# Five edits of order in a decoder layer: attention's beginning, halves of x, local maxima, up projection, merge

## What is computed

```python
z = x @ w_in
qa, ka, va, qi, ki, wi, qb, kb, vb, gate = jnp.split(z, SPLIT_POINTS, axis=-1)
ya = sparse_attention(...)          # 8 heads of 64, top-256 keys of an index score, T5 bias
yb = sliding_window_attention(...)  # 8 heads, 2 key-value heads, window 128, sinks, T5 bias
g = jax.nn.sigmoid(gate)
mix = (g[..., :D] * (ya @ w_pa) + g[..., D:] * (yb @ w_pb)) @ w_o
x = layer_norm(ALPHA * x + mix, ln1_g, ln1_b)
u = x @ w_up                        # 6144 columns: 3072 gate, 3072 value
c = conv_b + causal depthwise convolution of width 3 of u along the positions
x = layer_norm(ALPHA * x + (jax.nn.gelu(c[gate]) * c[value]) @ w_down, ln2_g, ln2_b)
```

## Time and profile before

| | |
|---|---|
| time, median of 3 runs | 3416.0 us (3415.43 to 3418.09) |
| profiled execution | 3410.55 us, span 3408.8 us |
| TensorE busy | 3252.1 us, 95% |
| VectorE busy | 2460.3 us, 72% |
| ScalarE busy | 1661.9 us, 49% |
| GpSimd busy | 1012.2 us, 30% |
| mean granted TensorE clock | 0.984 of full |

### The profile page before, as it was taken

The page is one execution under the profiler, slowest core; times in us unless marked ns, Lnnn a source line. Parts: engine busy times, 40 slices in busy tenths (PEclk is TensorE's granted clock), DMA queues, the critical chain, the costliest instruction groups (busy, mean ns, idle before and its releaser), DMA issues.

```text
span 3408.8 us, 40734 instructions
## 1 busy us (share of the span) xinstructions
PE 3252.1 (95%) x14552; PEld 2581.5 (76%) x14552; DVE 2460.3 (72%) x3632; ACT 1661.9 (49%) x2289; POOL 1012.2 (30%) x592
## 2 busy tenths in 40 slices
PE   7999989996899999999999999999999999999998
PEld 5788878874566666667877787777788888888887
DVE  5899999956566656446666799999899998343344
ACT  5669888215566676663222344444544444321211
POOL 1012232324466666650021144332233331000000
PEclk9999999997999999999999999999999999999999
DMA  6323333444232221035565322223322223533522
GB/s 172 59 75 99 99 105 99 134 162 96 74 77 70 60 65 49 7 110 193 176 247 185 119 87 100 105 101 133 108 92 75 93 87 128 197 103 117 173 96 95
DMA packets 219187, 376.81 MB, mean 111 GB/s; under 512 B 30573, under 2 KB 119933, under 8 KB 211182
## 3 DMA queue, kind: packets, MB, share of 16 engines
q1 hardware_dynamic: 217934, 369.86, 34.0%
q0 software_dynamic: 1056, 4.36, 0.3%
HBM read 276.24 MB, written 97.80 MB: 110 GB/s over the span
## 4 chain that ended last, share of the span: by engine, by line
PE 48%; DVE 16%; issue 6%; ACT 5%; DMA 2%; POOL 1%; SPq 1%; DVEq 0%; ACTq 0%; POOLq 0%
PE rs_ps L88 11%; PE rs_ps L90 11%; PE rs_ps L89 11%; DVE m_ul L1650 3%; DVE m_cval L1695 2%; PE rs_ps L1995 2%; PE rs_ps L1996 2%; PE rs_ps L2022 2%; PE rs_ps L1951 2%; PE rs_ps L2024 2%; PE rs_ps L2023 2%; PE rs_ps L1998 2%; DVE m_cval L1694 2%; ACT m_cval L1383 1%; DVE m_cg L1694 1%
## 5 line engine op out<-in xcount | busy, mean ns | idle before, releaser
L88 PE MATMUL rs_ps<-m_xh,m_uh 128*128 128x512 f32 x1344 | 529.1, 394 | 10.4 <-DVE m_u L1671 5.5
L90 PE MATMUL rs_ps<-m_xh,m_ul 128*128 128x512 f32 x1344 | 524.4, 390 | 0.0
L89 PE MATMUL rs_ps<-m_xl,m_uh 128*128 128x512 f32 x1344 | 524.3, 390 | 0.0
L1145 POOL TENSOR_TENSOR plo<-pf,phi 128x1024 fp32r<-128x1024 f32 x168 | 401.9, 2394 | 268.3 <-ACT phi L1252 262.9
L88 PE MATMUL frt_acc<-frt_xh,frt_wh 128*128 128x512 f32 x864 | 338.6, 392 | 11.0 <-issue 6.6
L90 PE MATMUL frt_acc<-frt_xh,frt_wl 128*128 128x512 f32 x864 | 338.5, 392 | 0.0
L89 PE MATMUL frt_acc<-frt_xl,frt_wh 128*128 128x512 f32 x864 | 338.4, 392 | 0.0
L88 PEld LDWEIGHTS rs_ps<-m_xh,m_uh 128*128 128x128 f32 x1344 | 253.1, 188 | 75.8 <-DVE m_ul L1650 20.5
L88 PE MATMUL rs_ps<-m_wh,m_hh 128*128 128x512 f32 x768 | 299.7, 390 | 2.0 <-DVE m_u L1685 2.0
L90 PE MATMUL rs_ps<-m_wh,m_hl 128*128 128x512 f32 x768 | 299.4, 390 | 0.0
L89 PE MATMUL rs_ps<-m_wlo,m_hh 128*128 128x512 f32 x768 | 299.3, 390 | 0.0
(11 more groups left out here) (290 smaller groups left out, 7572.2 us busy)
## 6 DMA issues: line engine op xcount, KB each, us to landing
m_ur<-in_w_up_dram SPq DMA_DIRECT2D x48, 1024.0 KB, 4.8
m_wr<-in_w_down_dram SPq DMA_DIRECT2D x60, 512.0 KB, 4.7
zt<-frt_out SPq DMA_DIRECT2D x108, 256.0 KB, 4.7
frt_wr<-in_w_main_dram SPq DMA_DIRECT2D x51, 512.0 KB, 4.3
ht<-m_cg SPq DMA_DIRECT2D x48, 512.0 KB, 2.6
m_hr<-ht SPq DMA_DIRECT2D x96, 256.0 KB, 3.4
m_raw<-zt SPq DMA_DIRECT2D x64, 256.0 KB, 4.1
m_sg<-zt SPq DMA_DIRECT2D x64, 256.0 KB, 4.5
```

Source lines behind the costliest of these rows:

```text
L88: pe.matmul(out, ahi, bhi, start=first, stop=False)
L89: pe.matmul(out, ahi, blo, start=False, stop=False)
L90: return pe.matmul(out, alo, bhi, start=False, stop=last)
L1145: pool.tensor_tensor(plo[:, k % PS, :], pf[:, k % PS, :], f32(phi[:, k % PS, :]), ALU.subtract).then_inc(S["pl"], 1)
```

## The change

- *Input projection:* in the groups of three items the two halves of x are gone through in turn, so that three items share a half before the other half begins (the very first group in an order of its own). The reload of the first half of x waits for a new semaphore `xf` (the half's last use), that of the second for the last item. TensorE waits for each half by itself. The planner's due times of `lx` and `x` count from the end of the half, and the one of the rounding of weight tile NT - 1 is 5 us behind its release and not 7.
- *Attention's beginning:* `prepare` is gone. Its keys' low part and casts stand in VectorE's prologue, the values' low parts stay at the first `max`, and the low part of the second bias (`low_sink`) comes at the second `max`. The copy of the sinks and the rounding of the second bias are ScalarE's, after the first `exponential`; the rounding of the first bias is in ScalarE's prologue. `bq` of the window bias has its two 128-column halves swapped.
- *Local maxima:* a `top` of a window block is one matmul of 512 columns (the bias of two heads by the identity, weights `idb`) and one of 256 columns per head (query by both key blocks at once), instead of eight of 128.
- *Up projection:* `value(r - 1)` of round r becomes `value(r - 2)` behind the first sums, before `conv(r - 1, 0)`; `low(r + 1, 1)` moves behind the sums of the values. In round 23 SP issues two row loads before the hidden store.
- *Merge:* the stores of the third and fourth row of `x1` come two units later (m == 2), and `norm1(3, 3)` stands behind `low_x(0, 4, ...)`.

```diff
...
@@ -162,10 +162,19 @@
         x_load = [2 + a for l, a in items]
         final = [max(j for j in range(NM) if items[j][0] == l) for l in range(NL)]
-        x_free = {2: None, 3: None, 4: max(j for j in range(NM) if x_load[j] == 2), 5: max(j for j in range(NM) if x_load[j] == 3)}
+        x_free = {i: max(j for j in range(NM) if x_load[j] == i - 2) for i in (4, 5)}
 
         plan = [("x", 0, 0), ("iw", 0, 0), ("x", 0, 1), ("iw", 1, 0), ("x", 1, 0), ("x", 1, 1)]
-        fill, todo = [], [(j, k) for j in range(NM) for k in range(KT)]
+        turned = {last * 2 + 3 * g for g in range(4)}
+        fill, todo, j = [], [], 0
+        while j < NM:
+            if j not in turned:
+                todo += [(j, k) for k in range(KT)]
+                j += 1
+                continue
+            halves = ((0, 0), (1, 0), (0, 1), (1, 1), (2, 0), (2, 1)) if j == 2 * last else ((0, 0), (1, 0), (2, 0), (0, 1), (1, 1), (2, 1))
+            todo += [(j + i, 4 * h + k) for i, h in halves for k in range(4)]
+            j += 3
 
@@ -194,23 +203,25 @@
             todo = todo[2:]
             dclock = max(dclock, clock) + 3.1 * work[g][2] / CH + 0.2
-        ends = [0.0] * NM
+        ends, half_end = [0.0] * NM, {}
         for t, (op, j, k) in at:
             if op == "main":
                 ends[j] = t
+                half_end[j, k // 4] = t
         for j, k in todo:
             clock += 0.685
             at.append((clock, ("main", j, k)))
             ends[j] = clock
+            half_end[j, k // 4] = clock
         for j in range(NM):
             at.append((ends[j] + 4.0, ("evict", j, 0)))
         for l in range(RW, NL):
             at.append((ends[final[l - RW]] + 0.01, ("lw", l, 0)))
-            at.append((ends[final[l - RW]] + (5.0 if l == NT else 7.0), ("w", l, 0)))
+            at.append((ends[final[l - RW]] + (5.0 if l >= NT - 1 and l <= NT else 7.0), ("w", l, 0)))
         for i in (4, 5):
             for h in range(2):
-                at.append((ends[x_free[i]] + 0.02, ("lx", i, h)))
-                at.append((ends[x_free[i]] + 9.0 + 2.0 * h, ("x", i, h)))
+                at.append((half_end[x_free[i], h] + 0.02, ("lx", i, h)))
+                at.append((half_end[x_free[i], h] + 8.0, ("x", i, h)))
         start = dclock + 24.0
@@ -237,6 +248,8 @@
                 if i == 2 or i == 3:
                     sp.wait_ge(S["cm"], 3 * (i - 1))
+                elif i >= 4 and h == 0:
+                    sp.wait_ge(S["xf"], i - 3)
                 elif i >= 4:
@@ -552,12 +565,12 @@
                 l, a = items[j]
                 r = l % RW
+                if x_load[j] >= 4 and k % 4 == 0:
+                    pe.wait_ge(S["xlp"], 2 * (x_load[j] - 4) + k // 4 + 1)
                 if k == 0:
                     pe.wait_ge(S["wld"], l + 1)
                     if x_load[j] < 4:
                         pe.wait_ge(S["xld"], 2 * (x_load[j] + 1))
-                    else:
-                        pe.wait_ge(S["xlp"], 2 * (x_load[j] - 3))
                     if j < 3:
@@ -568,6 +581,8 @@
                 if k == KT - 1:
                     ins.then_inc(S["mm"], 1)
+                if k == 3 and j in x_free.values():
+                    ins.then_inc(S["xf"], 1)
 
...
@@ -985,7 +1000,7 @@
                     if u + R < NU:
                         load_unit(u + R)
-                    if q and m == 0:
+                    if q and m == 2:
                         store_mid(q - 1, 2)
@@ -1066,11 +1081,11 @@
                     load_down(2)
                     load_down(3)
-                if r:
-                    store_hidden(r - 1)
                 if r == NS - 1:
                     load_rows(1, 4)
                     load_rows(1, 5)
+                if r:
+                    store_hidden(r - 1)
             for n in range(4, 8):
@@ -1210,11 +1225,15 @@
             def round_near(kind):
                 if kind:
-                    act.wait_ge(S["rnd"], 3)
+                    act.wait_ge(S["lsn"], 16)
+                    act.activation(near[0:1, 1, 1, :].rearrange("p (h q) -> p h q", h=HEADS),
+                                   snk[0:1].rearrange("p (h o) -> p h o", o=1).broadcast_to([1, HEADS, P]), ACT.Copy).then_inc(S["skd"], 1)
+                    act.wait_ge(S["skd"], 1)
                 act.activation(bhi[:, kind], near[:, kind], ACT.Copy).then_inc(S["bhd"], 1)
 
             for half in range(2):
                 act.activation(khh[half * DH:(half + 1) * DH], kva[0:DH], ACT.Copy).then_inc(S["kr"], 1)
+            round_near(0)
 
@@ -1290,16 +1309,15 @@
                     queries(b)
                 elif op == "top" and (b, x) == (0, (0, 0)):
-                    round_near(0)
                     round_values()
-                elif op == "max" and b == 0:
-                    round_near(1)
                 elif op == "kv":
                     window_keys(seq[b][1])
                 elif op == "vt":
                     window_values(seq[b][1])
                 elif op == "logits":
                     exponential(first[b] + x)
+                    if b == 0:
+                        round_near(1)
                 elif op == "finish":
@@ -1498,19 +1516,17 @@
                               ident[0:HEADS, 0:HEADS].rearrange("p (h o) -> p h o", o=1).broadcast_to([HEADS, HEADS, P]),
                               -1.0, None, ALU.mult).then_inc(S["cst"], 1)
-            dve.tensor_copy(bq[:, 1], nearq[:, 1]).then_inc(S["rnd"], 1)
-            dve.wait_ge(S["cst"], 2)
-
-            def prepare():
+            dve.tensor_copy(idr[:], ident[:]).then_inc(S["cst"], 1)
+            dve.wait_ge(S["kr"], 1)
+            dve.tensor_tensor(klo[0:DH], kva[0:DH], f32(khh[0:DH]), ALU.subtract).then_inc(S["kdone"], 1)
+            dve.tensor_copy(irep[:].rearrange("p (a b) -> p a b", a=4),
+                            ident[:].rearrange("p (a b) -> p a b", a=1).broadcast_to([P, 4, P])).then_inc(S["cst"], 1)
+            dve.tensor_copy(bq[:, 1, :, 0:P], nearq[:, 1, :, P:2 * P])
+            dve.tensor_copy(bq[:, 1, :, P:2 * P], nearq[:, 1, :, 0:P]).then_inc(S["rnd"], 1)
+            dve.wait_ge(S["cst"], 4)
+
+            def low_sink():
                 dve.wait_ge(S["lsn"], 16)
-                dve.tensor_copy(near[0:1, 1, 1, :].rearrange("p (h q) -> p h q", h=HEADS),
-                                snk[0:1].rearrange("p (h o) -> p h o", o=1).broadcast_to([1, HEADS, P])).then_inc(S["rnd"], 1)
-                dve.wait_ge(S["kr"], 1)
-                dve.tensor_tensor(klo[0:DH], kva[0:DH], f32(khh[0:DH]), ALU.subtract).then_inc(S["kdone"], 1)
-                low_values()
-                dve.tensor_copy(idr[:], ident[:]).then_inc(S["cst"], 1)
-                dve.tensor_copy(irep[:].rearrange("p (a b) -> p a b", a=4),
-                                ident[:].rearrange("p (a b) -> p a b", a=1).broadcast_to([P, 4, P])).then_inc(S["cst"], 1)
                 dve.wait_ge(S["bhd"], 2)
@@ -1745,7 +1761,9 @@
                     negmax(b)
                     if b == 0:
-                        prepare()
+                        low_values()
+                    elif b == 1:
+                        low_sink()
                 elif op == "spread":
@@ -1812,9 +1830,9 @@
             norm1(NQ - 1, 2)
             low_x(0, 3, 1)
-            norm1(NQ - 1, 3)
             low_x(0, 4, 0)
             low_x(0, 4, 1)
+            norm1(NQ - 1, 3)
             low(1, 1)
@@ -1834,14 +1852,14 @@
                     low_down(2)
                     sum_values(r - 1)
+                if r > 1:
+                    value(r - 2)
                 if r != NS - 1:
                     conv(r - 1, 0)
                 if r == NS:
                     low_x(1, 5, 0)
                 if r < NK:
                     low(r, 6)
-                if more:
-                    low(r + 1, 1)
                 if r == NS - 1:
@@ -1858,6 +1876,7 @@
                     low_x(1, 6, 0)
                 if more:
+                    low(r + 1, 1)
                     low(r + 1, 0)
@@ -1865,7 +1884,6 @@
                 elif r == NS:
                     low_x(1, 6, 1)
-                value(r - 1)
                 if more:
@@ -1885,6 +1903,7 @@
                     low_down(0)
                     low_down(1)
+            value(NK - 1)
             for n in range(3, ND):
@@ -1937,14 +1956,16 @@
                     pe.wait_ge(S["rnd"], 2)
                     pe.wait_ge(S["kd"], n + 1)
-                    w = P * min(2, n + 1)
+                    here, back = n % 2, 2 + (n - 1) % 3
+                    if n:
+                        keys = khb[:, here:back + 1:back - here, h // 4, :]
+                        pe.matmul(sq[:, r, :], idb[:], bq[:, 1, h:h + 2, :].rearrange("p a b -> p (a b)"), start=True, stop=False)
+                    else:
+                        keys = khb[:, 0, h // 4, :]
+                        pe.matmul(sq[:, r, :].rearrange("p (a b) -> p a b", a=2)[:, :, 0:P], idb[:], bq[:, 1, h:h + 2, 0:P], start=True, stop=False)
```

(8 more changed lines are left out.)

4 lines of the change are left out of this document (2 added, 2 removed).

## The result

The changed kernel took 3389.8 us (median of four runs, 3384.0 to 3393.4) against 3417.05 for the kernel before beside it: 0.9924 of it, 95% interval 0.9904 to 0.9944, that is 26 us faster. Forecast were 50 us and 3366, between 3348 and 3390. The sign was right, the size was half, and the time lies at the upper edge of that range.

A forecast was written before the change was run, and what follows sets the result against it. TensorE, computing 95% of the span, was taken as the bound, with VectorE setting the pace in the up projection's slow rounds. Gains 19 + 6 + 12 + 3 + 7 + 3 = 50 us gave 3366 against the median, range 3348 to 3390.

The forecast's parts named there:

- The rounds: Up projection's slow rounds: moved product and low part fill VectorE's two holes, rounds fall to 19.0 to 19.3 us; gain 19.
- the rival on the slower side: Up projection: weights loaded behind the hidden store come too late, TensorE waits in 46 rounds; 3418 us and more, chance 0.05.
- that of VectorE staying the bound: Up projection rounds: moved pieces meet GpSimd's work and grow, so 17 of 19 us are lost; 3388 us, chance 0.13.
- The turn: Up projection, rounds 22 to 24: VectorE arrives on time after shorter rounds; gain 6 us, between 1 and 10.
- which makes up for the store's being later: Turn, queue SP: two row loads passing the hidden store were said to offset that store's delay; no size given.
- Local maxima: Attention's window blocks: fewer, wider matmuls shorten sixty groups from 0.66 or 0.75 to 0.45 or 0.50 us; gain 12, 4 to 18.
- VectorE's reduction, 0.69 us per group: Local maxima: VectorE's pace for several groups in a row, limiting the gain to 4 us if it held for all.
- the port pair: Ports VectorE shares with GpSimd, an exclusive lock; named as the mechanism for moved up projection pieces growing, giving 3388 us.
- Attention's beginning: Window maxima begin some 10.5 us earlier, 5.5 given back through ScalarE's chain; taken as 3 us gain, between -1 and 6.
- which had been a bound: Attention's beginning: GpSimd's low part of bias 0, some 4.8 us, might hold VectorE's first queries and leave no gain.
- Exchange: Input projection, x by halves: stops at x go, a stop of about 2.6 us at weights comes; net 7, 0 to 13.
- Merge: norm1(3,3) behind low_x(0,4) shortens transposes' waits, later x1 stores let unit loads pass; gain 3 us, between 0 and 4.5.

The follow-up runs named there:

- run 12: Changed kernel with six corrections plus, at the turn, ScalarE's rounding and VectorE's low part of the first transposed rows earlier: 3363.4 us, 0.9854 of the kernel before.
- run 4: Changed kernel with the last row load, load_rows(1, 6), issued ahead of the hidden store: 3381.8 us.
- run 11: Changed kernel with six corrections, but the local maxima narrow again, eight matmuls of 128 columns: 3375.8 us, 0.9893 of the kernel before.
- run 2: Kernel before with the wider local maxima alone: 3410.8 us against 3413.45, ratio 0.9988.
- run 5: Changed kernel with the window maxima's last step as a reduction over pairs (maximum, sink) in one small tile instead of a two-operand comparison: 3383.7 us.
- run 6: Changed kernel with the low part of the second bias behind the spread of block 1: 3383.6 us.
- run 7: Changed kernel with GpSimd's low part of the first bias behind its memsets: 3384.2 us.
- runs 3 and 4: The first: changed kernel with stores of x1's third and fourth rows back at m == 0, 3383.3 us; the second: last row load ahead of hidden store, 3381.8 us.
- runs 5 and 9: The first: maxima's last step as reduction, 3383.7 us; the second: changed kernel with six corrections (stores, row load, last step, second bias, GpSimd order, last group), 3361.3 us.

## Why the prediction was right and wrong

**The rounds: right.** Forecast 19 us, measured 19.5 in the changed kernel and 20.0 alone, with rounds of 19.04 us. The holes were filled, and no load of weights came late: the rival on the slower side and that of VectorE staying the bound both fell. The latter gave 3388, close to the 3389.8 measured; that is chance, since the loss lies elsewhere. The down projection gave 2 us that no term held.

**The turn: the premise failed.** "VectorE comes to this place late, because its rounds before were too long." It did not. The sum (L1679/L1695) starts 3.5 us after the first matmul of the turn before (2375.86 against 2372.38) and 3.3 after the change (2354.55 against 2351.29), so shorter rounds ahead of it brought it no closer to TensorE. The transposes were to wait under 4 us in all and waited 12.1, where it had been 8.7. The stop of 4.7 us stands in the changed kernel as it did before, 4.9; run 12 shows that it is the order behind the sum. ScalarE's timeline of the changed kernel, where the transposed rows come last:

```profile
2355.27 0.20 ACT L1397 ACTIVATE m_halo<-m_uu 128x2 f32<-128x2 f32 x1 [2.25 <-DVE m_uu L1695]
2355.38 1.23 ACT L1401 ACTIVATE m_cg<-m_uu,m_cb,m_cw 128x1024 f32<-128x1024 f32 x1
...
2358.02 1.55 ACT L1366 ACTIVATE m_xh<-rs_ps 128x512 fp32r<-128x512 f32 x3
```

And the sentence that two row loads pass the store, "which makes up for the store's being later", left out the third, which stands behind it: 4.5 us (run 4) of a loss of 6.0 where a gain of 6 was forecast. These 12 us are the largest part of the 33 by which the profiles fall short of the forecast.

**Local maxima: the price was right, the place it went to was not seen.** The group came to 0.46 us, and 15.2 us for 60 (run 11) lie within the 10 to 18 of the columns; the forecast of 12 was even low. In the changed kernel the rest of attention gained only 5 us, and the maxima alone 4.3 (run 2). The step that failed is "VectorE's reduction, 0.69 us per group" as the thing that stands against it. What did was the next instruction, of 0.17 us, held for up to 2.3 us by GpSimd (run 5: 7.35 us, of which 6.6 in the rest of attention). The prediction named the port pair and looked for it in the up projection, where nothing came of it.

**Attention's beginning: right mechanism, larger on both sides.** The first logits came 8.1 us earlier. Of this 6.5 were given back behind them, 5.5 by the low part that waits for ScalarE (run 6), as forecast to the half microsecond, and GpSimd's low part took 3.7 (run 7), which had been a bound. Net 1.6, forecast 3.

**Exchange: right mechanism, too small in this profile.** The stops at x went and the one at item 60 came, 4.5 us for a forecast 2.6; the missing 1.9 is ScalarE's counts: it rounded the weights 6.3 us after the load's issue, against 4.5 in the chain of the earlier trace rows. With the stop at item 50 (2.8 us) the profile shows 5.2 us gained by item 60 and 2.8 by the projection's end (forecast 7), and the runs 3 and 4 without that stop 12.5 and 11.6 by item 60. Between item 60 and the projection's end 2.4 us go again, about what 5 us at half the clock cost behind the stop (last row of this document); the forecast had 1.7.

**Merge: wrong sign.** Forecast 3, measured a loss of 7.4 in this profile and of about 4 as a mean of the later stores. The clause "the larger stops there (7.8 us) wait for VectorE's L1590, whose order is untouched" reads the releaser and not what that one waited for: L1590 stands behind ScalarE and this behind the load. The rest of the 7.4 is not the stores'. In the first 82 us of the merge TensorE did 297 matmuls in the changed kernel and 309 before, at a mean clock of 0.94 and 0.98, which is some 3 us (12 x 0.2265, an estimate); the same stands in run 2, which has the old merge, and run 7 has the old count to within 2, so it comes and goes without an edit there. Its cause stays open. These are the rows (kernel before, then changed):

```profile
1518.00:1600.00 82.00, 73.36 (x309) 58.24 (x308) 55.98 (x69) 35.06 (x40) 4.14 (x3) 0.98 0.71 225
```

```profile
1509.00:1591.00 82.00, 72.92 (x297) 58.57 (x296) 54.28 (x67) 35.65 (x41) 3.58 (x3) 0.94 0.70 224
```

The smaller step, `norm1` behind `low_x`, gave nothing: 36.39 us from the first up projection matmul to the next round against 36.29, since the larger stop of the transposes only moved one group later, with 2.7 us instead of 2.4.

The sum of the measured terms: 19.5 - 6.0 + 5.0 + 1.6 + 2.8 - 7.4 + 2.0 = 17.5, against 17.1 between the two last matmuls.

## What to carry to other kernels

When work is made shorter on the engine that binds, list the small instructions behind it that have two operands in SBUF, and the copies, and see what GpSimd runs at their new time; here such a step could be written as a reduction of one tile, which was not held, while a copy of the same size was. When a queue entry is delayed, check every entry behind it. And a releaser in a row of waits is a place to read on from, to its own releaser, before its cost is called untouched.

## What the runs showed of the hardware that was not expected

- A VectorE instruction on eight numbers per partition took 2.32 us beside GpSimd, and the same result as a reduction of one tile 0.17 us at the same place and time (run 5).
- A VectorE copy of eight numbers per partition with one operand took up to 8.57 us beside GpSimd's subtraction and memsets, and 1.9 us for two beside a memset (runs 5 and 9).
- GpSimd's memsets did not hold VectorE's query, of two operands: it took 1.22 us at 772.89 with memsets running (run 7), and 4.87 us beside a subtraction (changed kernel). They did hold the copies.
- The exchange of x scatters without any change of code: the stretch from item 44 to 60 took 98.2, 98.2 and 98.1 us in three profiles, 95.9 in one and 90.9 and 91.8 in two, all with the same projection. The difference is mainly a stop at item 50 for the low weights (2.8 us in the first three, 1.8 in the fourth, none in the others), a shorter one before it, and the clock behind stops. What decides between the two stays open; ScalarE's counts, which stand ahead of these weights and wait for VectorE's search, are the nearest suspect and were not tried.
- The 0.66 of the earlier trace rows is a mean of the clock's two levels: within that window, from 463.2 to 466.4 us, it was 0.50, the lower one (1.2 of 2.4 GHz). Behind the stop of 4.5 us at item 60 it was 0.50 for 5 us on end. Windows of the kernel before, then of the changed one, columns as in the earlier trace rows:

```profile
463.20:466.40 3.20, 3.20 (x9) 2.47 (x8) 3.20 (x9) 3.20 (x5) 0.00 (x0) 0.50 0.97 315
```

```profile
496.00:501.00 5.00, 4.66 (x11) 3.72 (x12) 4.86 (x15) 4.01 (x6) 0.24 (x1) 0.50 0.12 48
```
